# Attention probabilities turned by products with diagonals of gate over sum, three branches summed in PSUM

## The reference, cut to what matters

```python
def masked_softmax(s, mask):
    s = jnp.where(mask, s.astype(jnp.float32), NEG_INF)
    m = jnp.max(s, axis=-1, keepdims=True)
    e = jnp.where(mask, jnp.exp(s - m), 0.0)
    return e / jnp.maximum(jnp.sum(e, axis=-1, keepdims=True), 1e-30)
...
    o_c, imp = nsa_cmp_attend(qb, t, kc, vc)            # compressed blocks
...
    o_s = gathered_attend(qb, kg, vg, (kpos <= t[None, None, :, None]) & ok)
...
    o_w = window_attend(qb, t, wb[:, :, 0], wb[:, :, 1], kpos_w)
    return gb[:, :, 0] * o_c + gb[:, :, 1] * o_s + gb[:, :, 2] * o_w
...
def mem_attend(q, mkv):
    s = jnp.einsum('bqhd,bmhd->bhqm', q, mkv[:, :, 0]) * SCALE
    p = jax.nn.softmax(s.astype(jnp.float32), axis=-1)
    return jnp.einsum('bhqm,bmhd->bqhd', p.astype(mkv.dtype), mkv[:, :, 1])
...
    mix = jnp.concatenate([
        o_n.astype(f32) * jax.nn.silu(z_n.astype(f32)),
        o_r.astype(f32) * jax.nn.silu(z_r.astype(f32)),
        o_m.reshape(B, T, MEM_W).astype(f32) * jax.nn.silu(z_m.astype(f32)),
    ], axis=-1).astype(x.dtype)
    return x + mix @ w_out
```

## Time and profile before

| | us |
|---|---|
| median of 3 runs | 937.1 (935.34 to 937.9) |
| the profiled execution | 935.25 |
| its span | 933.4 |
| attention part, from the first scores to the first output projections | about 478 to 830 |
| PE busy in 478 to 830 | 331.19 of 352 |
| PEld busy there | 275.58 |
| DVE, ACT, POOL busy there | 255.35, 231.47, 135.84 |
| granted TensorE clock there | 1.00 |

### The profile page before, as it was taken

How to read it: one execution, slowest core, us unless ns; L and a number is a source line. 1 busy time by engine, 2 the same in 40 slices (tenths; PEclk the granted TensorE clock), 3 DMA queues, 4 the chain that set the end, 5 groups by cost and what they waited for, 6 DMA issues and landing times.

```text
span 933.4 us, 20468 instructions
## 1 busy us (share of the span) xinstructions
PE 895.8 (96%) x7594; PEld 812.4 (87%) x7594; DVE 520.3 (56%) x1501; ACT 414.2 (44%) x1063; POOL 290.2 (31%) x497
## 2 busy tenths in 40 slices
PE   6999999999999999999999999999999999999997
PEld 6999999999999999999987788768877788778885
DVE  4656332422323275555656787676777758844443
ACT  6442221225344201111666666566765668832221
POOL 0223222222226344534144262334322626410000
PEclk9999999999999999999999999999999999999998
DMA  8554423415241544232869067715504142343331
GB/s 231 175 194 143 145 63 132 141 51 122 72 145 30 141 125 128 82 100 69 209 177 237 3 184 261 248 46 139 163 2 133 55 141 66 116 144 126 128 121 67
DMA packets 85220, 117.91 MB, mean 126 GB/s; under 512 B 12930, under 2 KB 67506, under 8 KB 84546
## 3 DMA queue, kind: packets, MB, share of 16 engines
q1 hardware_dynamic: 71666, 73.12, 27.5%
q0 software_dynamic: 10224, 36.20, 11.6%
q10 hardware_dynamic: 3232, 7.28, 2.2%
HBM read 91.50 MB, written 32.02 MB: 132 GB/s over the span
## 4 chain that ended last, share of the span: by engine, by line
PE 82%; DVE 5%; ACT 4%; issue 4%; DMA 2%; POOL 2%; ACTq 0%; SPq 0%; DVEq 0%; POOLq 0%
PE psum L601 9%; PE psum L602 8%; PE psum L603 8%; PE psum L1876 7%; PE psum L1755 5%; PE psum L1732 4%; PE psum L1897 3%; PE psum L1896 3%; PE psum L1895 3%; PE psum L1733 3%; PE psum L852 2%; ACT p_P L1985 2%; PE psum L854 2%; PE psum L853 2%; PE psum L588 2%
## 5 line engine op out<-in xcount | busy, mean ns | idle before, releaser
L601 PE MATMUL psum<-a_whi,f_xhi 128*128 128x256 f32 (+1 forms) x672 | 194.4, 289 | 1.6 <-DVE f_xlo L1077 1.4
L602 PE MATMUL psum<-a_wlo,f_xhi 128*128 128x256 f32 (+1 forms) x672 | 189.9, 283 | 0.0
L603 PE MATMUL psum<-a_whi,f_xlo 128*128 128x256 f32 (+1 forms) x672 | 189.5, 282 | 0.0
L1985 ACT ACTIVATE p_P<-psum,p_nb 128x640 f32<-128x640 f32 (+7 forms) x224 | 124.4, 562 | 46.1 <-DVE p_nb L2057 38.6
L601 PEld LDWEIGHTS psum<-a_whi,f_xhi 128*128 128x128 f32 x672 | 126.8, 189 | 4.0 <-DVE a_wlo L577 1.8
L602 PEld LDWEIGHTS psum<-a_wlo,f_xhi 128*128 128x128 f32 x672 | 127.1, 189 | 0.0
L603 PEld LDWEIGHTS psum<-a_whi,f_xlo 128*128 128x128 f32 x672 | 127.1, 189 | 0.0
L754 POOL DMA_DIRECT2D h_scratch<-a_hst x93 | 50.9, 549 | 232.4 <-DVE a_hst L1137 119.2
L1755 PE MATMUL psum<-f_ident,p_P 128*128 128x128 f32 x656 | 99.5, 275 | 1.4 <-ACT s_KTw L1935 0.8
L1755 PEld LDWEIGHTS psum<-f_ident,p_P 128*128 128x128 f32 x656 | 76.9, 141 | 8.1 <-DVE p_PT L1923 2.2
L2057 DVE CUSTOM_DVE_ANT_0 psum<-psum,p_near 128x256 f32<-128x256 f32 (+7 forms) x96 | 64.6, 673 | 32.8 <-PE psum L1733 27.1
(11 more groups left out here) (339 smaller groups left out, 2168.4 us busy)
## 6 DMA issues: line engine op xcount, KB each, us to landing
a_wraw<-in_w_in SPq DMA_DIRECT2D x24, 512.0 KB, 4.2
h_scratch<-a_hst POOLq DMA_DIRECT2D x72, 128.0 KB, 3.6
s_SG<-in_cache_nsa_slc SPq DMA_DIRECT2D x64, 128.0 KB, 2.3
p_qd<-q_scratch SPq DMA_DIRECT2D x16, 384.0 KB, 7.2
a_xraw<-in_x_prompt SPq DMA_DIRECT2D x8, 512.0 KB, 7.0
s_MK<-in_cache_mem SPq DMA_DIRECT2D x8, 512.0 KB, 9.2
s_WG<-in_cache_nsa_win SPq DMA_DIRECT2D x8, 512.0 KB, 5.1
mix_scratch<-p_zt POOLq DMA_DIRECT2D x8, 512.0 KB, 3.7
```

Source lines behind the costliest of these rows:

```text
L601: nc.tensor.matmul(out, hi, wh, start=first, stop=False)
L602: nc.tensor.matmul(out, hi, wl, start=False, stop=False)
L603: return nc.tensor.matmul(out, lo, wh, start=False, stop=last)
L1985: nc.scalar.activation(dst, s_view(s), ACT.Exp, bias=nb[:, g % NNB:g % NNB + 1], scale=1.0 if s[2] == 3 else -1.0, accum_out=ssum[:, par[i ...
```

## The change: what it does, and the diff

P is no longer transposed with the identity and scaled afterwards. Each turn is a product of a piece of P (stationary) with a diagonal matrix `DG` (moving), whose diagonal is the gate over the softmax's sum. The three branches then need no scaling, and `pv` sums them in one group of 128 columns of bank 7.

- POOL makes a diagonal for each of the 224 softmaxes (`pool_diagonals`, four buffers `DG`). `pool_gates`, `gw` and the additions of `pool_mix_group` go.
- DVE takes one reciprocal a unit (`rw` steps, 144). `normalize` becomes `mix`: it multiplies the turned output by z straight into `zt`.
- The turns of unit v are a unit later in the list, in the round of unit v + 1. P gets three buffers.
- A block's `OT` has 128 columns and two buffers, and chunk `o` has one transpose. The two memory units are blocks of their own: 6 blocks a tile, 48 in all.
- POOL's loads move: the gates of a tile a unit after the last unit of the tile before it in the same buffers, z seven units after (six before). The zeroing of the sample's tiles moves into unit 6.
- `gf` (final norm) has a place of its own and is loaded later.

```diff
@@ tiles @@
+    NRW = 8
+    NDG = 4
-    rw = rp("rw", [128, 2, 8])
+    rw = rp("rw", [128, NRW, 2])
-    OT = rp("OT", [128, 384])
-    Oi = [rp(f"Oi{i}", [128, 6, HD]) for i in range(2)]
+    P.append(rp("P2", [128, T]))
+    OTs = [rp("OT0", [128, 128])]
+    DG = [ru(f"DG{i}", [128, 128]) for i in range(NDG)]
+    OTs.append(ru("OT1", [128, 128]))
@@ schedule @@
-        z_at = {of_tile[prev[i]][-1] + 6: i for i in TILES[2:]}
+        z_at = {of_tile[prev[i]][-1] + 7: i for i in TILES[2:]}
+        z_at.update({1: FIRST, 9: SECOND})
+        g_at = {of_tile[prev[i]][-1] + 1: i for i in TILES[2:]}
...
-        for v in range(NV):
-            i, l = UNITS[v]
+        for v in range(NV + 1):
+            if v < NV:
+                steps.append(("rw", v))
             if v + 2 < NV:
                 steps.extend([("qk", v + 2), ("max", v + 2)])
...
+            if v > 0:
+                u, l = v - 1, UNITS[v - 1][1]
+                tiles = tiles_of(u)
...
+                    mine.append(add_p(u, tiles[f:f + 4]))
@@ PE @@
-                pe.wait_ge(S("p_exp"), sm_count(v) - len(sms) + 1 + tiles[-1][0])
+                pe.wait_ge(S("p_dg"), sms[tiles[-1][0]][0] + 1)
...
-                    l = nc.tensor.transpose(o[0:w, 128 * j:128 * j + 128], P[v % 2][:, at:at + w], ident[:])
+                    l = nc.tensor.matmul(o[0:w, 128 * j:128 * j + 128], P[v % 3][:, at:at + w], DG[sms[a][0] % NDG][:], start=True, stop=True)
...
-                for j in range((numbers(BLOCKS[n][1]).stop - numbers(BLOCKS[n][1]).start) // 2):
-                    l = nc.tensor.transpose(o[:, 128 * j:128 * j + 128], OT[:, 128 * j:128 * j + 128], ident[:])
+                l = nc.tensor.transpose(o[:, 0:128], OTs[n % 2][:], ident[:])
@@ ACT @@
-                if v >= 2:
-                    act.wait_ge(S("p_tr"), last_chunk[v - 2] + 1)
+                if v >= 3:
+                    act.wait_ge(S("p_tr"), last_chunk[v - 3] + 1)
@@ DVE @@
+        def weights(v):
...
+            dve.wait_ge(S("p_exp"), sm_count(v))
+            if v >= NRW:
+                dve.wait_ge(S("p_dg"), sm_count(v - NRW))
+            r = nc.vector.reciprocal(w, ssum[:, par[i], num:num + step * (n - 1) + 1:step])
...
+            r.then_inc(S("p_rw"), 1)
+        def mix(c):
...
+            nc.vector.tensor_tensor(z, bank(4 + c % 3)[:, 0:128].rearrange("p (j d) -> p j d", j=2), z, ALU.mult).then_inc(S("pt_dve"), 1)
@@ POOL @@
+    def pool_diagonals(pool, v):
+        i, l = UNITS[v]
+        pool.wait_ge(S("p_rw"), v + 1)
+        if v == of_tile[i][0]:
+            pool.wait_ge(S(f"p_g{par[i]}"), 16 * (rank[i] + 1))
+        for a, (g, num, b, h, *_) in enumerate(softmaxes(v)):
+            if g >= NDG:
+                pool.wait_ge(S("p_tr"), sm_chunk[g - NDG] + 1)
+            w = rw[:, v % NRW, a:a + 1]
+            if b == 3:
+                pool.tensor_scalar(DG[g % NDG][:], ident[:], w, None, ALU.mult).then_inc(S("p_dg"), 1)
+            else:
+                c = 8 * ((b + 1) % 3) + h
+                pool.tensor_scalar(DG[g % NDG][:], ident[:], w, gt[par[i]][:, c:c + 1], ALU.mult, ALU.mult).then_inc(S("p_dg"), 1)
```

More of the change, by code:

```diff
@@ L1476, in schedule @@
             for part in range(3):
-                free = of_tile[prev[i]][-1] - 1 if prev[i] is not None else 2
+                free = of_tile[prev[i]][-1] - 1 if prev[i] is not None else 3
                 v = max(of_tile[i][0] - 11 + 2 * part, free + part)
@@ L1484, in schedule @@
             steps.extend([("qk", v), ("max", v), ("sm", v)])
-        for v in range(NV):
-            i, l = UNITS[v]
+        for v in range(NV + 1):
+            if v < NV:
+                steps.append(("rw", v))
             if v + 2 < NV:
                 steps.extend([("qk", v + 2), ("max", v + 2)])
[L1489 to L1499, removed]
+            if v > 0:
+                u, l = v - 1, UNITS[v - 1][1]
+                tiles = tiles_of(u)
+                mine = []
+                for f in range(0, len(tiles), 4):
+                    mine.append(add_p(u, tiles[f:f + 4]))
+                    if l >= 16:
+                        waiting.append((mine[-1], mine[-1]))
+                    elif l % 2:
+                        waiting.append((partner[len(mine) - 1], mine[-1]))
+                partner = mine
+                while waiting and (l % 2 == 0 or l >= 16) and waiting[0][1] not in mine:
+                    pv()
             if v + 2 < NV:
                 steps.append(("sm", v + 2))
+            if v == NV:
+                break
+            if v in g_at:
+                steps.append(("load_g", g_at[v]))
             if v in z_at:
                 steps.append(("load_z", z_at[v]))
-            if v - 4 in z_at:
-                steps.append(("gates", z_at[v - 4]))
+            if v == 6:
+                steps.append(("zero", 0))
             for k, part in q_at.get(v, []):
@@ L1568, in build @@
     last_chunk = {p_chunks[c][1]: c for c in p_index}
+    sm_chunk = {softmaxes(p_chunks[c][1])[a][0]: c for c in p_index for a, _, _ in p_chunks[c][2]}
     x_last = {c[1]: k for k, c in enumerate(p_chunks) if c[0] == "x"}
@@ L1870, in pv @@
                     g = unit_block[vj]
-                    if j == 0 and k == 0 and num in (0, 6, 12, 18, 24) and g >= 1:
+                    first = k == 0 and b in (0, 3)
+                    if j == 0 and first and g >= 1:
                         pe.wait_ge(S("p_ot"), g)
-                    at = 512 * 7 + 128 * ((num - numbers(num // 6).start) // 2)
+                    at = 512 * 7
                     kv = HD * (h // 4)
@@ L1876, in pv @@
                     i_mm = nc.tensor.matmul(psum[64 * j:64 * j + 64, at:at + 128], val, PTs[p_rank[pair[j]] % NPT][0:w, 128 * p:128 * p + 128],
-                                            start=k == 0, stop=128 * (k + 1) >= keys, skip_group_check=True)
+                                            start=first, stop=b >= 2 and 128 * (k + 1) >= keys, skip_group_check=True)
             i_mm.then_inc(S("p_pv"), 1)
@@ L2001, in act_attend @@
             elif what == "ot":
-                c = numbers(BLOCKS[n][1])
                 act.wait_ge(S("p_pv"), ot_pv[n])
-                if n >= 1:
-                    act.wait_ge(S("p_tr"), place["o", n - 1] + 1)
-                nc.scalar.copy(OT[:, 0:64 * (c.stop - c.start)], bank(7, 64 * (c.stop - c.start))).then_inc(S("p_ot"), 1)
+                if n >= 2:
+                    act.wait_ge(S("p_tr"), place["o", n - 2] + 1)
+                nc.scalar.copy(OTs[n % 2][:], bank(7, 128)).then_inc(S("p_ot"), 1)
             elif what == "copy_win":
@@ L2151, in dve_attend @@
                     if kind == "o":
-                        normalize(n)
+                        mix(n)
                     elif kind == "p":
@@ L2160, in dve_attend @@
                         sample_chunk(n)
-            elif what == "ot":
+            elif what == "rw":
                 weights(n)
@@ L2266, in pool_attend, with load_g @@
         pool.wait_ge(S("h_mm"), len(proj_jobs))
-        for i in range(2):
-            pool.memset(P[i][:, 704:768], 0.0).then_inc(S("p_zero"), 1)
-        wait_stored(pool, len(proj_jobs) - 1)
+        wait_stored(pool, last_job[5])
+        def load_g(i):
+            if prev[i] is not None:
+                pool.wait_ge(S("p_dg"), sm_count(of_tile[prev[i]][-1]))
+            pool.dma_start(gt[par[i]][:], hD[128 * i:128 * i + 128, C_G:C_G + 24]).then_inc(S(f"p_g{par[i]}"), 16)
         def load_z(i):
```

139 lines of the change are left out of this document (58 added, 81 removed).

## The result

The changed kernel takes **1005.6 us** (median of 4 runs, 1004.75 to 1005.96). The kernel before, in the same rounds, takes 936.3 (935.34 to 937.9). The ratio is 1.074, with a 95% interval of 1.0725 to 1.0756: **69 us slower**. The forecast was 992 us, the range 968 to 1022. The range holds the time, 13.6 us above the forecast.

The account below looks back on a forecast made before the run. The prediction took PE to bound the kernel. From the profiled 935.25 us it added 67.9 for turns and 10 for POOL, and took off 7.0 for output turns and 14 for waits: 992 us, range 968 to 1022.

Parts of the forecast that it names:

- turns, work of PE: PE, attention part: 656 turns become float32 products of two records, 0.2125 us in place of 0.109, +67.9 us.
- waits given back: PE, attention part: longer turns cover part of at most 29 us of real waits, -14 us.
- output turns and the new order: PE: 112 transposes of the sums become 48, -7.0 us; the later turn and third P buffer cancel for exp.
- POOL's diagonals: PE waits for diagonals queued behind POOL's DMA waits: 6 us at z's load, 2 at sample's mix, 2 at start, +10.
- the half: Half of PE's 29 us of waits given back, as the four tiles with few keys keep theirs: -14 us.
- the price of a switch of column width: PE's weight load: 0.17 us per switch between full and half column width products, 8.0 and 12.4 us in all.
- a real wait: PE's weight load: what is left of an unnamed wait after the switch price, 6.9 us of 14.9.
- cancels for exp: PE's scores waiting for exp: third P buffer and turn a unit later offset each other, so that way gets no longer.
- A: Turn on PE: product with a diagonal costs what the transpose does, 0.109 us, so not slower, 928 us; 3%.
- B: PE's waits: all 29 us go under the longer turns and POOL's stalls do not come, 967 us; 15%.
- C: POOL sets the pace: full stalls of 27 us and no wait given back, 1023 us; 12%.
- D: Turn on PE: four passes, four times the transpose's cost, POOL hidden altogether, 1113 us; 2%.

Follow-up runs that it names:

- the product alone: The kernel before with only its turning transposes replaced by plain float32 products with the identity, in the old order: 986.8 us, ratio 1.0551.
- behind exp, with product: The changed kernel with turns as products with the identity, waiting for exp and not for POOL's diagonals, which are made unused: 989.6 us.
- F32R run: The changed kernel with P and the diagonals declared as F32R, at lower precision of the weights: 974.4 us, ratio 1.0422.
- the run with transposes: The changed kernel with turns made by transposes with the identity, diagonals still made and awaited, gates and sums left out of the result: 972.7 us.
- with short turns: The changed kernel turned by transposes with the identity that wait for exp and not for the diagonals, gates and sums left out: 944.3 us.
- the run that removes it: The changed kernel with the steps of the sample's mix four groups further behind their load: 996.7 us, ratio 1.0659.

## Why the prediction came out as it did

| step | predicted | measured | from |
|---|---|---|---|
| turns, work of PE | +67.9 | +75 | 0.224 against 0.109 us, 656 times |
| waits given back | -14 | -24 | the product alone, +51 in place of +75 |
| output turns and the new order | -7.0 | +3 | behind exp, with product: 989.6 - 986.8 |
| POOL's diagonals | +10 | +16 | 1005.6 - 989.6 |
| sum over the kernel before | +57 | +70 | measured +69 |

**The turns.** Two records a call, in a dense row some 0.11 us apart: right in kind. The size was read from 16 records of the trunk, 0.106 us; the eight of L1231 have 64 moving columns and not 128, and the other eight give 0.1075. The turns took 0.112, just over the slowest row of the trunk (0.110). The term was 7 us too small. The F32R run shows that it is the second record that costs: 656 records again, and the time of the run with transposes. The Trainium skill's rule of four (TensorE: Matmul & The Clock Gate, Terms) does not hold in this kernel: the trace gives 0.224 against 0.109, a factor of 2.05.

**The waits given back.** The forecast took half of 29 us, because it thought the units with few turns would keep theirs. 24 went, or 22.9 by the starts of PE's records. The step that failed is the half. The waits for exp fell by half as foretold, from 13.7 to 7.4 us. But 10.4 us came back around the output turns and the sample's steps, of which the 29 held only the longer waits. Of the two rows named "issue" the forecast took 47 and 73 times 0.17 us as the price of a switch of column width, and fixed. At the values this holds on PE: the distance from the last turn is 0.20 us as before, though the row fell from 15.9 to 2.9. At the scores the price is more than 0.17: of the 6.9 us called a real wait only 1.1 went, and 13.8 us in 47 places stayed.

**The output turns and the order.** -7.0 had been forecast for this. With the product, the new order instead costs 2.8 us over the old one, about what the scatter allows. 3.2 of it is the zeroing of P's edge behind the gates' load, which the forecast did not see: it spoke of the start only as one more round to fill. That leaves 6.6 us between -7.0 and -0.4 that no run isolates. PE's starts say that what begins with an output turn took 4.6 us less, and not 7.0, and that the sample's steps behind turns and values cost 1.7 more; the rest stays open. That the order "cancels for exp" is not shown: with short turns the waits for exp grew from 13.7 to 22.0 us.

**POOL.** The diagonals took 0.446 us with two factors, as forecast (0.46), and 0.60 with one, a mean over only 32. POOL sets no pace; PE waits for it in ten places, not in most units. The mechanism was right, a DMA wait with diagonals queued behind it, and the places were the ones named. Their sizes were the other way round: 2.1 us at the load of z, where 6 were forecast, since the landing took 15.0 us at most (the row below, which answers to the earlier trace rows) and PE came later; and 8.9 at the sample's mix, where 2 were forecast. There the wait of 8.23 us became 10.62, where the forecast thought that POOL would come later, and of 10.62 us PE lost 6.93: the stock covered 3.7 us, and two rounds of 2.8 had been counted on. The other waits of PE for a diagonal are short, 5.3 us in eight places.

```profile
DMA to landing us min/median/max: 2.4/3.6/15.0
```

**What no term had.** Behind these stalls the granted clock fell. This cost 2.1 us at the start, by the same 80 records in two traces, and about 2 at the mix, by the run that removes it. It could be seen in the kernel before: the 1.00 of its attention part is rounded, and behind the wait at the load of z (2.05 us on PE, 2.26 on PEld) it has this stretch:

```profile
597.00:601.00 4.00, 4.00 (x27) 3.39 (x27) 2.78 (x8) 1.96 (x7) 0.00 (x0) 0.57 0.91 304
```

The rivals: *A* falls by the 1312 records. *B* was nearer on the waits, 24 of its 29, and fails on POOL. *C* had POOL's loss about halfway to its 27 us and fails on the waits. *D* falls by the 0.224. The errors were +7 (turns), -10 (waits), +10 (order and start) and +6 (POOL), 13 in all with the sign of "slower". That the time came within 13.6 us of the forecast is in part luck: the error of the waits and that of the order cancel.

## What to carry to other kernels

Before a transpose is folded into a product to save work on other engines, count the records: here a plain float32 product has two where the transpose has one, and on the engine that is the bound this is paid in full, less what waits it covers. An engine put on the way of the bound must not have a DMA wait in its list just ahead of what the bound needs; move such a step behind its load by some rounds, and look again, since too late is a wait as well. Costs measured one at a time do not add up where work hides waits: here 51 and 37 us made 69.

## What the runs showed of the hardware

- The clock after a stall. PE stood for 6.93 us, and then took 2.47 us for ten records that otherwise take 1.28, a factor of 1.9. In the stretch from 484 to 488 us, behind the stall of 3.42 that ended at 481.82, the mean granted clock was 0.56, near the lower of the two levels (1.2 and 2.4 GHz); with the stall cut to 1.28 us, the products behind it ran at full length, 0.41 us instead of 0.64.

```profile
484.00:488.00 4.00, 4.00 (x21) 3.98 (x21) 1.78 (x10) 1.82 (x6) 2.10 (x4) 0.56 0.80 257
```

- An F32R product of 128 x 128 has one record, as a transpose has, and stands about as long: 0.112 against 0.109 us (656 records, 974.4 against 972.7 us).
- Values behind turns start 0.20 us after the last turn, whether the turns are transposes or products (medians 0.203 and 0.205), while PEld's idle there is 0.17 us behind transposes and 0.12 behind float32 products.
- GpSimd multiplies a 128 x 128 tile by two per-partition factors in 0.446 us, no longer than the 0.49 of a tensor_tensor of that size.
